# Scores of the next round taken in front of the turnings, in each step of an attention stage whose matmuls are one hand-written order

## The reference, cut to what matters

```
sc = einsum(q, k) * scale                      # blocks of 128 queries
pr = softmax(where(chunk mask, sc, lowest))    # keys of the same or an earlier 64-chunk
a  = pr[:, :, 0] - lam * pr[:, :, 1]           # the two heads of a pair
out = einsum(a, v)                             # (128 queries) x (keys) x 128
m = sigmoid(g_att + b0) * (rmsnorm(out) * silu(z_att)) @ w_att_out + sigmoid(g_conv + b1) * y_conv
x + rmsnorm(m @ w_out)
```

## Time and profile before

| | us |
|---|---|
| median of 3 runs | 1772.46 |
| lowest and highest run | 1770.55, 1774.26 |
| the profiled execution, its own time | 1767.66 |
| its span (first to last instruction) | 1765.8 |
| TensorE busy in the span | 1741.4 |
| VectorE busy in the span | 890.1 |
| from 736 to 1410: TensorE busy | 665.93 |
| from 736 to 1410: VectorE busy | 446.47 |
| from 736 to 1410: ScalarE busy | 316.90 |

### The profile page before, as it was taken

The page is one execution under the profiler, slowest core; times in us unless marked ns, Lnnn a source line. Parts: engine busy times, 40 slices in busy tenths (PEclk is TensorE's granted clock), DMA queues, the critical chain, the costliest instruction groups (busy, mean ns, idle before and its releaser), DMA issues.

```text
span 1765.8 us, 22477 instructions
## 1 busy us (share of the span) xinstructions
PE 1741.4 (99%) x8512; PEld 1459.0 (83%) x8512; DVE 890.1 (50%) x1895; ACT 585.0 (33%) x1040; POOL 109.4 (6%) x82
## 2 busy tenths in 40 slices
PE   7999999999999999999999999999999999999998
PEld 6888888888888888888888887888888888888887
DVE  5536334444433611267767665767766453424242
ACT  5422112121101211244444444444444442323231
POOL 0000000000000000110101112111001040000000
PEclk9999999999999999999999999999999999999999
DMA  6545746465503445975666669658576875353532
GB/s 238 150 165 224 276 167 211 170 203 179 179 24 110 153 119 145 310 230 186 198 203 207 203 212 289 193 178 229 197 226 186 273 267 186 113 179 107 185 107 72
DMA packets 164678, 328.90 MB, mean 186 GB/s; under 512 B 15569, under 2 KB 60625, under 8 KB 159185
## 3 DMA queue, kind: packets, MB, share of 16 engines
q1 hardware_dynamic: 164562, 327.38, 58.7%
HBM read 216.16 MB, written 111.16 MB: 185 GB/s over the span
## 4 chain that ended last, share of the span: by engine, by line
PE 92%; DMA 4%; DVE 1%; SPq 1%; issue 1%; ACT 1%; DVEq 0%; ACTq 0%
PE bank L970 19%; PE bank L972 19%; PE bank L971 19%; PE bank L1100 17%; PE bank L1060 5%; PE bank L1032 3%; PE bank L1033 3%; PE bank L1043 3%; DMA q_st<-qk_s 1%; DMA z_in<-z_s 1%; DMA ring<-gate_s 1%; PE bank L980 1%; PE bank L1080 1%; PE bank L1077 1%; DMA qk_s<-stage 1%
## 5 line engine op out<-in xcount | busy, mean ns | idle before, releaser
L970 PE MATMUL bank<-ht,w 128*128 128x512 f32 x896 | 348.6, 389 | 0.0
L971 PE MATMUL bank<-ht,w 128*128 128x512 f32 x896 | 348.6, 389 | 0.0
L972 PE MATMUL bank<-ht,w 128*128 128x512 f32 x896 | 348.5, 389 | 0.0
L1100 PE MATMUL bank<-ht,w 128*128 128x512 f32 x912 | 236.9, 394 | 0.0
L972 PEld LDWEIGHTS bank<-ht,w 128*128 128x128 f32 x896 | 168.2, 188 | 34.9
L971 PEld LDWEIGHTS bank<-ht,w 128*128 128x128 f32 x896 | 168.2, 188 | 34.9
L970 PEld LDWEIGHTS bank<-ht,w 128*128 128x128 f32 x896 | 168.2, 188 | 34.9
L1100 PEld LDWEIGHTS bank<-ht,w 128*128 128x128 f32 x912 | 166.3, 188 | 31.8
L1632 DVE CUSTOM_DVE_ANT_0 e<-bank,zeros 128x512 f32<-128x512 f32 x192 | 124.9, 688 | 132.6 <-PE bank L1033 132.2
L1312 ACT ACTIVATE e<-e,nbias 128x128 f32<-128x128 f32 (+15 forms) x128 | 153.7, 1201 | 69.8 <-DVE nbias L1641 69.6
L1100 PE MATMUL bank<-hx,w 128*128 128x512 f32 x576 | 153.9, 394 | 0.0
(11 more groups left out here) (140 smaller groups left out, 2507.9 us busy)
## 6 DMA issues: line engine op xcount, KB each, us to landing
w<-split_s SPq DMA_DIRECT2D x124, 512.0 KB, 4.9
split_s<-piece SPq DMA_DIRECT2D x24, 1024.0 KB, 5.0
q_st<-qk_s SPq DMA_DIRECT2D x128, 128.0 KB, 5.0
gate_s<-gate_st SPq DMA_DIRECT2D x64, 256.0 KB, 5.2
ring<-gate_s SPq DMA_DIRECT2D x64, 256.0 KB, 3.4
raw<-in_w_in SPq DMA_DIRECT2D x28, 512.0 KB, 6.1
ht_s<-ht SPq DMA_DIRECT2D x3, 4096.0 KB, 15.8
qk_s<-stage SPq DMA_DIRECT2D x48, 192.0 KB
```

The source lines that it names most:

```text
L970: nc.tensor.matmul(out, left[0], right[0], start=start, stop=False)
L971: nc.tensor.matmul(out, left[0], right[1], start=False, stop=False)
L972: return nc.tensor.matmul(out, left[1], right[0], start=False, stop=stop)
L1100: mm = nc.tensor.matmul(bank[2 + u % 2][:], unit_weights(u)[:, term // 2, k, :], h_slot(bb, k)[:, term % 2, :], start=i == 0, stop=i == PE ...
```

## The change

In the loop of TensorE's program the two `if` blocks for the scores and for the turnings change places. Nothing else differs: the instructions, their waits, the programs of the other engines and the plan are the same.

```diff
                     for j, (turned_part, scored_part, value_part, part) in enumerate(steps):
-                        if turned_part:
-                            turn(R - 1, *turned_part)
                         if scored_part:
                             for h in range(2):
                                 score(R + 1, *scored_part, h)
+                        if turned_part:
+                            turn(R - 1, *turned_part)
                         if value_part:
                             values(R - 1, *value_part)
```

## The result

| | before | after |
|---|---|---|
| median of 20 runs, us | 1770.66 | 1775.8 |
| lowest and highest run | 1767.49, 1774.26 | 1771.73, 1778.0 |
| the profiled execution, its own time | 1767.66 | 1776.34 |
| its span | 1765.8 | 1774.5 |

The ratio of after to before, taken between runs on the same chip, is 1.0025, with a 95% interval of 1.0018 to 1.0033. On 1770.66 that is 4.4 us slower (3.2 to 5.8); the two medians are 5.1 apart. The forecast was 6.15 us slower. Of these 2.8, 1.8 is the start: the 3 runs' median lay that much above the median of 20.

A forecast was written before the change was run, and what follows sets the result against it. The prediction took TensorE, busy 99% of the span, as the bound, with small waits for VectorE. Its terms, 2.94 + 2.77 + 0.33 + 0.11 = 6.15 us, on 1772.46 gave 1778.6 us, range 1773.5 to 1783.5.

The forecast's parts named there:

- TensorE is the bound, and waits for at_lo are what moves: Attention: TensorE sets the end; its weight loads' waits for at_lo rise from 10.5 us to some 16 us.
- No time of TensorE's own: TensorE, 146 steps: reordering scores and turnings costs zero; it may save 1.5 us or, unlikely, cost 12 us.
- Mask_max waits for the turnings: VectorE, each step: head 0's mask_max waits for its scores and for the turnings that read the buffer it overwrites.
- It is 0.48 late: VectorE, each step: mask_max starts 0.47 to 0.48 us later, behind head 1's scores, and at_lo ends 0.48 later.
- The list of rounds: Even rounds whose values wait for at_lo: delay less cover adds 2.94 us up to round 30, 2.77 in rounds 33 to 64.
- Round 64: Rounds 33 to 64 were taken as the same plan again, 2.77 us in all; no term was given for round 64.
- Round 20's third chunk: Round 20: the third chunk already waits for at_lo and its mask_max is late by 0.48, making the round's sum 0.48.
- The queries, 0.33 and 0.11: Rounds 3 and 33: turnings now stand behind the first score's wait for queries, adding 0.33 and 0.11 us.
- VectorE isn't late: Rival, even rounds 18 to 30 and 50 to 60: mask_max goes by its scores alone; 3.9 us faster, 1768.6; chance 0.05.
- The handover costs: Rival, TensorE: score to turning or turning to value costs 0.03 x 146 = 4 us more, 1782.6; chance 0.10.
- The transfers absorb it: Rival, rounds 3, 32 and 33: shifted transfer waits absorb most of 4.0 us; 1774.6, no measurable change; chance 0.17.
- The delay is less than it looks: Rival: missed cover or a quicker signal halves the terms; 3.1 us above before, 1775.5; chance 0.13.

The follow-up runs named there:

- even_rounds: Scores put in front of the turnings in even rounds alone, odd rounds as in the kernel before; 1774.45 us, +3.7 us against before, ratio 1.0021.
- queries_earlier: The changed kernel with the queries' load asked for earlier, ahead of one step's gate loads; 1768.11 us, -3.5 us against before, ratio 0.9980.
- odd_rounds: Scores put in front of the turnings in odd rounds alone, even rounds as in the kernel before; 1771.07 us, +0.5 us against before, ratio 1.0003.
- head1_first: The changed kernel with head 1 first, its mask_max not waiting for the turnings; 1769.01 us, -1.4 us against before, ratio 0.9992.
- more_cover: The changed kernel with the plan's weight for values 5 instead of 6, giving even rounds more gates; 1770.99 us, -0.9 us against before, ratio 0.9995.
- between_heads: The changed kernel with the turnings moved between the scores of head 0 and head 1; 1770.39 us, +0.2 us against before, ratio 1.0001.
- more_cover_turns_first: The kernel before, turnings in front, with the plan's weight for values 5 instead of 6; 1768.63 us, -2.3 us against before, ratio 0.9987.

## Why the prediction was right, and by which step its size was off

- **TensorE is the bound, and waits for at_lo are what moves:** right. L1060 waits 3.9 us more, where some 5.5 more were forecast, in 23 places for about 25. The 3.9 of the weight loads and not the 1.9 of the matmul rows is near the 3.70 that the starts give.
- **No time of TensorE's own:** right, and a little better than zero. The stated test was a stretch in which the waits don't change; rounds 4 to 18 are one. In before round 4 starts at 758.84 and round 19 at 949.85, 191.01 us apart; in after the same starts are 759.13 and 949.83, 190.70 apart. So 0.31 us is gained in these fifteen rounds, and 0.7 in the whole attention. The prediction had named such a saving, up to 1.5, and taken zero. The cost of up to 0.08 for a step isn't there. From the last 512-wide score matmul to the first turning it is 0.23 (1012.06 to 1012.29), as from gate to turning.
- **Mask_max waits for the turnings:** right, in 113 places.
- **It is 0.48 late:** this is the term that was mis-sized. It is 0.31 late. The sum for it was 0.94 of scores, 0.60 of turnings and 0.17 for the signal. The scores took 0.91 and the turnings' row 0.60, but VectorE started 0.04 behind that row's end (1012.89 to 1012.93), not 0.17. The 0.17 had been read behind a 512-wide score's row. What lies between a matmul row's end and the consumer's start is thus no property of the signal; it differs with the kind of matmul. The Trainium skill (Perfetto Trace Analysis, Tensor Engine Instruction (MATMUL, LD_WEIGHTS)) has it that the end of a TensorE row is estimated from the instruction's size and is not measured. The trace agrees, with 0.04 behind one form and 0.17 behind another.
- **The list of rounds:** right but for rounds 14 and 16 (and their repeats 46 and 48), where 0.04 was expected and the smaller delay stayed under the cover. The others came out at 0.19 to 0.33 each where I had 0.17 to 0.48. In all 1.94 in rounds 2 to 30 (forecast 2.94) and 1.76 behind (forecast 2.77): 3.70 for 5.71, in the trace. Even_rounds and queries_earlier have the same increments in their own traces, within 0.03 for each quiet even round, and odd_rounds none. The pair with queries earlier gives 3.2 us in the times.
- **Round 64** was put at nothing, and it came out 0.86 longer. There VectorE waits for its z_in load, and the values behind it for at_lo. It comes again in even_rounds (1.25) and queries_earlier (0.80), and in no kernel with the turnings in front by more than 0.32; but head1_first and more_cover haven't got it either. So it may be part of the change's steady price; that is not shown.
- **Round 20's third chunk** waits 0.37 for at_lo where it had waited 0.23, and round 32's wait, which hangs on a transfer, is 1.29 for 1.34, as supposed.
- **The queries, 0.33 and 0.11:** not borne out term by term. In round 3 the wait was 0.41 for 0.98 and the round came out 0.5 shorter; in round 33 it was 1.44 longer, and the clock fell. "If the waits for transfers change by more than 2 us" I had called my forecast wrong, and in the one profiled execution, with the clock behind them, they did. It isn't the rule over the runs: 4.4 us by the ratio less 3.2 for at_lo leaves 1.2, and this lies within the intervals. The other profiles say that the longer wait is not the order's. In the nine kernels whose load stands at its old place the wait in round 33 was 1.71, 2.05, 2.23, 2.36, 2.41, 2.75, 2.93, 3.15 and 3.27 us; before has the shortest, and even_rounds, which takes the turnings first in round 33 as before does, the longest. Nor is it the clock: the mean granted clock of after's 20 runs is 0.9988, and that of before's runs beside the experiments 0.9986 to 0.9989. Whether the 1.2 is round 64 or nothing is open.
- **The rivals.** "VectorE isn't late" is refuted by the 113 places, and head1_first shows what it would have taken. "The handover costs" is refuted by the level stretch and odd_rounds. "The transfers absorb it" did not happen. "The delay is less than it looks" had been priced at 3.1 us; the truth, 4.4, lies about midway between it and the forecast, for its second reason, a quicker signal. That the median of the runs, 1775.8, falls on that rival's 1775.5 is partly luck, as the start was 1.8 too high.

## What to carry to other kernels

When two blocks of one engine's order change places, list what each consumer waits for, and look for a wait on the block that goes back: here it was a buffer's reuse and not the data itself. Then price the delay only where a consumer behind it has less cover: here in 13 of 64 rounds. Measure a signal behind the same kind of instruction, from a start and not from a modelled end. And ask whether the order within the waiting engine can be chosen so that the work that doesn't need the block goes first: with it the change's 4.4 us were gone. Where the consumer waits already, a little more cover helps both orders alike and leaves the difference, here 2.8 us in the quiet even rounds. Last, follow a wait for a transfer to the load that it waits for, here one asked for two rounds before, and not to the load that happens to be issued beside it.

## What the runs showed of the hardware that was not expected

- **A wait can cost twice, but need not.** In a stretch in which TensorE was busy 0.85 of 4 us the granted clock fell 1.1 us before the 3.15 us wait ended, and behind it it was 0.53 for 6 us, worth 2.8 us. In between_heads it was 0.72 over 6 us behind a 2.75 us wait, and in more_cover_turns_first, too, it fell, behind one of 2.93. Behind the waits of 1.71 to 2.41 us in five kernels it stayed at 1.00, but so it did behind the longest, 3.27 us in even_rounds, with 0.73 us busy of 4:

```profile
1073.00:1077.00 4.00, 0.73 (x5) 0.51 (x4) 0.00 (x0) 0.88 (x4) 0.00 (x0) 1.00 1.06 339
1077.00:1083.00 6.00, 6.00 (x32) 5.07 (x31) 3.38 (x14) 2.36 (x7) 0.72 (x1) 1.00 1.06 295
```

  So the wait's length alone doesn't decide it. The Trainium skill (TensorE: Matmul & The Clock Gate, What's actually happening) has it that the clock is at its half or at its full rate and at nothing between. The trace of after agrees: read in half microseconds, the clock is 0.50 from 1075.0 to 1081.5 and 1.00 from 1082.0 on.
- **The queries' load is worth more than its waits.** The two waits in the profile of before are 2.7 us, and moving the load earlier in that order gave 6.7 (4.4 to 8.9). Two things go with that. The profile of before had the shortest wait of the nine in round 33, and it took 3.0 us less than its kernel's median. And the clock recorded for each run is a little lower with the load at its old place: on the chip of these runs 13 of before's 30 had 0.998 or less, and 1 of the 19 of the two kernels with queries earlier; the means are 0.9986 and 0.9993, which makes some 1 us over the span, by estimate. The rest is open: no slower execution of before was profiled.
- **Turnings need not be dear next to wide matmuls.** Four float32 transposes of 128 columns take 0.36 to the start of the next matmul (1012.29 to 1012.65). With three gates of 0.23 behind them the next score starts at 1013.43, so they take 1.14 less 0.69, 0.45, in all, beside 0.44 in the old order.
